# Which slots of a 128-slot tile the tokens of an expert take

## The reference

```python
g_idx = argmax(h @ w_grp + b_grp)                 # one of 4 groups for a token
e_prob = softmax(expert logits of that group)     # 8 experts in a group
top_p, top_local = lax.top_k(e_prob, 2)           # two experts for a token
order = jnp.argsort(expert); xs = h[order // 2]
a = ragged_dot(xs, w1, sizes); b = ragged_dot(xs, w3, sizes)
y = ragged_dot(silu(a) * b, w2, sizes) * weights[order][:, None]
return segment_sum(y, order // 2, num_segments=N) # each token gets its two rows back
```

## Time and profile before

| | us |
|---|---|
| median of three runs | 3200.97 |
| profiled execution | 3206.26 |
| its span, first to last instruction | 3204.0 |
| expert tiles within it, from the first gather to the end | 2560 to 3204 |

### The profile page before, as it was taken

One profiled execution on the slowest core, in us unless ns is written; L12 is line 12 of the kernel. 1 busy time (PEld: TensorE's weight loads), 2 busy tenths in 40 slices (PEclk: granted clock), 3 DMA queues, 4 the chain that ended last, 5 costly groups with the idle time before them and its releaser, 6 DMA issues. The chain is left out here.

```text
span 3204.0 us, 35751 instructions
## 1 busy us (share of the span) xinstructions
PE 2786.6 (87%) x13124; PEld 2228.3 (70%) x13124; DVE 2194.8 (69%) x2950; ACT 1271.2 (40%) x2069; POOL 858.3 (27%) x398
## 2 busy tenths in 40 slices
PE   6999999979588879789889968879599589999998
PEld 3777777755366668668777846768487478877776
DVE  5599975526698845844626978852544479888887
ACT  3222221110267621122324115666322167777775
POOL 1432310000111100001200025454321036776674
PEclk9999999989788889889999989989799589999999
DMA  6333347634455361235543255120532389999996
GB/s 217 99 109 116 106 162 250 200 120 141 152 188 187 128 246 53 87 99 118 118 120 76 76 130 101 38 50 18 219 118 93 132 313 380 364 362 355 365 360 218
DMA packets 244344, 543.37 MB, mean 170 GB/s; under 512 B 31109, under 2 KB 153973, under 8 KB 227906
## 3 DMA queue, kind: packets, MB, share of 16 engines
q1 hardware_dynamic: 174034, 436.42, 39.3%
q0 software_dynamic: 33840, 59.49, 7.4%
q10 hardware_dynamic: 36288, 45.09, 4.0%
HBM read 450.68 MB, written 108.06 MB: 174 GB/s over the span
## 5 line engine op out<-in xcount | busy, mean ns | idle before, releaser
L2548 DVE TENSOR_TENSOR e_low<-e_raw,e_high 128x4096 fp32r<-128x4096 f32 x99 | 441.7, 4463 | 87.5 <-ACT e_high L2542 87.4
L2542 ACT ACTIVATE e_high<-e_raw 128x4096 fp32r<-128x4096 f32 x99 | 359.5, 3634 | 138.0 <-DMA e_raw<-in_exp_w 111.0
L135 PE MATMUL banks<-h_high,w 128*128 128x512 f32 (+1 forms) x1088 | 309.1, 368 | 9.1 <-POOL w L364 4.4
L135 PE MATMUL banks<-p_w_high,p_high 128*128 128x512 f32 (+1 forms) x640 | 250.7, 392 | 14.7 <-DVE p_w_low L1593 14.7
L135 PE MATMUL banks<-p_w_low,p_high 128*128 128x512 f32 (+1 forms) x640 | 246.9, 386 | 0.0
L135 PE MATMUL banks<-p_w_high,p_low 128*128 128x512 f32 (+1 forms) x640 | 246.6, 385 | 0.0
L135 PE MATMUL banks<-e_high,e_xhigh 128*128 128x512 f32 x528 | 213.5, 404 | 26.4 <-issue 24.4
L135 PEld LDWEIGHTS banks<-h_high,w 128*128 128x128 f32 x1088 | 195.5, 190 | 48.6 <-POOL w L364 4.8
L495 DVE SCALAR_TENSOR_TENSOR acc<-img,taps,acc 128x1024 f32<-128x1024 f32 x160 | 209.8, 1311 | 5.7
L135 PE MATMUL banks<-e_high,e_xlow 128*128 128x512 f32 x528 | 208.5, 395 | 0.0
L135 PE MATMUL banks<-e_low,e_xhigh 128*128 128x512 f32 x528 | 208.0, 394 | 0.0
(11 more groups left out here) (501 smaller groups left out, 6598.3 us busy)
## 6 DMA issues: line engine op xcount, KB each, us to landing
e_raw<-in_exp_w SPq DMA_DIRECT2D x99, 2048.0 KB, 16.2
s_sums<-cumT SPq DMA_DIRECT2D x32, 768.0 KB, 4.4
w_raw<-in_w_in SPq DMA_DIRECT2D x20, 1024.0 KB, 6.6
s_X<-xtok SPq DMA_DIRECT2D x19, 1024.0 KB, 7.7
p_raw<-in_w_in SPq DMA_DIRECT2D x18, 1024.0 KB, 7.0
xbcT<-res ACTq DMA_DIRECT2D x20, 640.0 KB, 2.9
xtok<-xt ACTq DMA_DIRECT2D x20, 640.0 KB, 4.1
w_raw<-in_ada_w SPq DMA_DIRECT2D x12, 1024.0 KB, 5.4
```

What stands on the lines that cost most here:

```text
L135: last = pe.matmul(out, a, b, start=start and n == 0, stop=stop and n == len(pairs) - 1)
L2542: act.activation(self.high[p % HIGHS][:], self.raw[p % RAWS][:], ACT.Copy).then_inc(*self.high_done.up())
L2548: dve.tensor_tensor(self.low[p % HIGHS][:], self.raw[p % RAWS][:], self.high[p % HIGHS][:].bitcast(F32), ALU.subtract).then_inc(*self.low_ ...
```

## The change

A new row of 128 constants, `spread`, comes from memory to all partitions with the three others, and `here` compares it with `row_of` in place of the counting row. `spread[f(r)] = r`, where f(r) = 8 (r mod 16) + (r // 16 + (r mod 16) // 2) mod 8. So the token of rank r goes to partition f(r): ranks 0, 1, 2, 3, ... go to 0, 8, 17, 25, 34, 42, 51, 59, 68, ... Sixteen tokens that follow each other lie in sixteen different blocks of 8 partitions. The list, the slot weights, the gather and the scatter all go by the same `here`. The counting row is now only needed for tile numbers, and shrinks from 128 to 48 columns (`tile_numbers`).

```diff
+            "spread": np.argsort(8 * (k % 16) + (k // 16 + k % 16 // 2) % 8).astype(np.float32),
...
-        bgr, bex, cst, rows_in = rows
+        bgr, bex, cst, spread, rows_in = rows
...
-        token_no, token, line = new("token_no", NT), s.sb("r_token", [P, NT], I32), s.sb("r_line", [P, P], I32)
-        row_no = new("row_no", P)
+        token_no, token, line = new("token_no", NT), s.sb("r_token", [P, NT], I32), s.sb("r_line", [P, SLOT_TILES], I32)
+        tile_numbers = new("tile_numbers", SLOT_TILES)
...
-        pool.iota(line[:], [[1, P]], base=0, channel_multiplier=0).then_inc(*numbered.up())
+        pool.iota(line[:], [[1, SLOT_TILES]], base=0, channel_multiplier=0).then_inc(*numbered.up())
...
-        dve.wait_ge(*rows_in.at(3))
+        dve.wait_ge(*rows_in.at(4))
...
-        done(dve.tensor_copy(row_no[:], line[:]))
+        done(dve.tensor_copy(tile_numbers[:], line[:]))
...
-            done(dve.tensor_tensor(there[:, some, :], over(row_no[:, 0:SLOT_TILES], 1, NT), over(tile_of[:, j, :], 2, SLOT_TILES), ALU.is_equal))
+            done(dve.tensor_tensor(there[:, some, :], over(tile_numbers[:], 1, NT), over(tile_of[:, j, :], 2, SLOT_TILES), ALU.is_equal))
...
-            dve.tensor_tensor(here[:, some, :], over(row_no[:], 1, NT), over(row_of[:, j, :], 2, P), ALU.is_equal).then_inc(*placed.up())
+            dve.tensor_tensor(here[:, some, :], over(spread[:], 1, NT), over(row_of[:, j, :], 2, P), ALU.is_equal).then_inc(*placed.up())
...
+        spread = s.sb("r_spread", [P, P])
...
-            for to, name in ((bgr, "router_b_grp_2"), (bex, "router_b_exp_2"), (cst, "counts")):
+            for to, name in ((bgr, "router_b_grp_2"), (bex, "router_b_exp_2"), (cst, "counts"), (spread, "spread")):
```

More of the change, by code:

```diff
@@ L2820, in late @@
         slot_there = flat2(g)[:, 0:2 * NT * SLOT_TILES].rearrange("p (a n) -> p a n", n=SLOT_TILES)
-        route(core, dram, tables, (bgr, bex, cst, rows_in), lambda: [weights.fetch(m, j, m) for m, j in weights.order[0:3]], here, slot_there, weighed)
+        route(core, dram, tables, (bgr, bex, cst, spread, rows_in), lambda: [weights.fetch(m, j, m) for m, j in weights.order[0:3]], here, slot_there, weighed)
         experts(core, dram, tables, weights, y, g, dram["mod2"][0, 5 * D:6 * D], weighed)
```

## The result

The changed kernel takes 3176.3 us, the median of four runs (3173.68 to 3181.36), against 3201.6 us for four runs of the kernel before. The ratio is 0.9923, 95% interval 0.9906 to 0.9940. The forecast was 3177.5 us.

A forecast was written before the change was run, and what follows sets the result against it. DMA was taken to bound 23 of the 33 tiles, TensorE the rest. Terms -25.1 + 2 - 0.5 = -23.6 us, from 3201.0, gave 3177.4, stated as 3177.5; range 3174 to 3182, chance 0.66.

The forecast's parts named there:

- 23 tiles: Expert tiles from about 2731 us on: each goes from DMA's 18.86 us to TensorE's 17.77, -25.1 us.
- Eight engines carry the rows, and the excess in the shares is waiting: Expert tiles: eight engines carry all gathered and scattered rows; 8.7% excess in the weights' queue is waiting, not slower memory.
- Which group belongs to which engine: Token places: four partitions and four 32 further on give 17.81 us a tile after the change, 18.86 before.
- The price of a token: Gather and scatter: one row each per token, 0.525 us of engine time together, the empty slots' share included.
- pieces that come late: Weight pieces in the expert tiles: some late by a little, +2 us, bounds 0 and 6.
- last scatter: End of the kernel, tile of 7 tokens: two rows fewer in sequence, -0.5 us, bounds 0 and 1.3.
- fourth row, shorter counting row: Constants load and routing: the extra row is covered, the shorter row's saving lost in a wait; 0 us.
- the piece of lead in the raw buffers: First seven DMA-fed tiles: the piece in the raw buffers gives 7.6 us of lead, paying for DMA slightly over TensorE.
- Memory as the limit, hard or at 370 GB/s: Expert tiles: hard limit, no change, 3201, within a shared chance of 0.08; at 370 GB/s 3189, chance 0.09.
- Two engines still bound: Expert tiles: the fullest engine differs from tile to tile and still sets the pace; 3181 to 3187, chance 0.12.
- Partitions dealt out in turn: Token places: partitions go to engines in turn, so no change, 3201; within a shared chance of 0.08.
- The scatter's landing as the bound: Expert tiles: the next scatter waits for a landing that grows to 19.0 us; slower, 3213, chance 0.05.

The follow-up runs named there:

- e1: The changed kernel with the constants row holding 0, 1, 2, ..., so tokens fill partitions 0 to n - 1 as before; ratio to the kernel before 1.0003.
- e3: The changed kernel with places even by the rule of four partitions and four 32 further on; ratio to the kernel before 0.9921.
- d1: The changed kernel without low-part expert products, low part formed for half a piece, tokens in count order as before the change; 3194.1 us.
- d3: The changed kernel without low-part expert products, low part formed for half a piece, places even by four and four 32 further on; 3129.6 us.
- e2: The changed kernel without the rotation, rank r going to partition 8 (r mod 16) + r // 16; 3196.2 us, ratio to the kernel before 0.9978.
- d4_no_rows: The changed kernel without low-part expert products, low part formed for half a piece, every slot marked empty so no row moves; 3071.7 us.
- d2_change: The changed kernel, its token order kept, without low-part expert products and with the low part formed for half a piece; 3163.6 us.
- e4_no_rows: The changed kernel with every slot marked empty, so gathers and scatters move no row, all TensorE work kept; 3176.21 us, ratio 0.9907.

## Why the prediction was right

*What bounds.* DMA bounded 23 tiles at 18.86 us and TensorE would bound them at 17.77. After the change the same 23 tiles take 17.77.

*Eight engines carry the rows, and the excess in the shares is waiting.* The first part is shown by e1 to e3 and by d1 to d3, where only places differ. The second is shown by d1 to d3 as well: with the same bytes the recorded time of a weight row falls from 0.678 us to 0.620 when the rows are spread, and weights alone have 0.619. The prediction's count of it, from the kernel before alone, holds.

*Which group belongs to which engine.* The prediction took four partitions and four 32 further on, by a difference of 0.1 us for a tile. That was thin: with eight in a row the first sum would have been 18.97 against a measured 18.86. e2 and e3 separate the two rules by 20 us of the kernel's time in opposite directions, and both came out as this one says. The Trainium skill, page "DMA: Bandwidth & Descriptors", section "The descriptor swizzle", gives this rule for a transfer to 128 partitions, and all orders tried here agree with it for indirect ones. No run tries gather and scatter apart, but 0.52 us for a token is the recorded time of both its rows.

*The price of a token.* The 0.525 us hold the empty slots too. In d4_no_rows these take 1.1% of 16 engines, or 0.16 us a tile whatever the order, which is about what 14.90 us lie above the 14.77 of the prediction. The two small errors, a floor too low and a price too high, nearly cancel in the sums.

*The sum.* The stage from ScalarE's first weight piece went from 646.6 us (2557.38 to 3204.0) to 620.2 (2552.35 to 3172.5), so by 26.5, and the medians by 25.3. Term by term:

| term | predicted | measured |
|---|---|---|
| 23 tiles | -25.1 | -25.1 |
| pieces that come late | +2 | 0 |
| last scatter | -0.5 | -0.9 |
| fourth row, shorter counting row | 0 | 0 |
| before the first full tile | 0 | -0.5 |

The +2 was the one guess, and it was not needed. DMA alone takes 17.90 us in the change's order (d2_change), 0.13 over TensorE, which is 2.9 us in 22 tiles; the piece of lead in the raw buffers covers that. The lead can be followed in the change. Weight pieces land later after their issue in the middle of the tiles (2900 to 2950 us) than at their start (2610 to 2660):

```profile
e_raw<-in_exp_w SPq DMA_DIRECT2D x9, 2048.0 KB, 9.9
```

```profile
e_raw<-in_exp_w SPq DMA_DIRECT2D x9, 2048.0 KB, 12.2
```

In e4_no_rows it is 9.7 and 8.8 us in the same stretches, so it is the rows that use the lead up. After that it rises no more (12.0 us from 3050 to 3100), and no piece came late. Fuller tiles, or more of them, might show the 0.13 us; no run here has them. Here e3_by_fours would have room of 1.1 us for a tile and the change none. The 5 us by which the profiled spans differ beyond this lie ahead of the stage, where both kernels run the same instructions. The kernel by fours, with the change's code, has its first L2621 at 2589.9 us, the change at 2584.2 and the kernel before at 2589.5, so that part is scatter between executions.

*The rivals.* Memory as the limit, hard or at 370 GB/s: out (d3, d4). Two engines still bound: out for the kernel, though 17.90 shows how near it was. Partitions dealt out in turn: out (e1, which that rule would put at TensorE's 17.77 us a tile). The scatter's landing as the bound: it fell from 16.7 to 16.0 us, as forecast, and GpSimd's wait for it was 4.8 us in four places. With e3_by_fours that wait was 8.5 us in seven places, and still cost nothing. But the size of the landing was misread. I took it for turns behind weight packets and for rows. The last section shows that some 3.5 us of it are GpSimd's own, and in d4_no_rows a scatter that moves no row still lands 10.4 us after its issue at the median, against 12.4 in d2_change.

## What to carry to other kernels

An indirect DMA with many empty rows loads only the engines whose partitions hold the full ones; beside a stream that needs all 16, the fullest engine sets the pace, and spreading the rows costs one row of constants. Here that was 18.93 us a tile with 7.8 tokens on the fullest engine and 16.68 with 4.3. Check the order against the rule of four and four 32 further on: an order that was even in blocks of eight still used half of the engines for a tile of up to 64 tokens, and gained 0.2% instead of 0.8%. A DMA share of 0.98 is no proof of full engines, since e4_no_rows shows 0.96 at 83% of the rate: divide the GB/s by the rate in a stretch where nothing else runs.

## What the hardware showed beside this

GpSimd takes 5 us to issue a scatter beside VectorE's subtraction over 4096 columns, and 1.59 us when that is out of its way. Timeline of the changed kernel:

```profile
2806.67 4.42 DVE L2549 TENSOR_TENSOR e_low<-e_raw,e_high 128x4096 fp32r<-128x4096 f32 x1 [0.46 <-ACT e_high L2543]
2807.59 4.97 POOL L2680 DMA_INDIRECT result<-e_y,ids  x1 [0.89 <-POOL e_y L2676]
```

and of d2_change, where the subtraction is half as long and the issue falls between two of them:

```profile
2810.29 2.29 DVE L2549 TENSOR_TENSOR e_low<-e_raw,e_high 128x2048 fp32r<-128x2048 f32 x1 [2.70 <-ACT e_high L2543]
...
2814.61 1.59 POOL L2680 DMA_INDIRECT result<-e_y,ids  x1 [0.88 <-POOL e_y L2676]
2816.49 2.29 DVE L2549 TENSOR_TENSOR e_low<-e_raw,e_high 128x2048 fp32r<-128x2048 f32 x1 [3.25 <-ACT e_high L2543]
```

The scatters of that stretch of d2_change, duration and landing:

```profile
L2680 POOL DMA_INDIRECT result<-e_y,ids x22: 1588/1592/1595, 2743.9 to 3120.9; - x22
...
DMA to landing us min/median/max: 11.6/12.4/12.9
```

The issue never takes more than 1.6 us there, and the median landing falls from 16.0 to 12.4 us, though DMA is as full as before. In the changed kernel the issue ends at 2812.56 us, 1.47 us after the end of the subtraction (2811.09), so nearly a whole undisturbed issue lies behind that end. It looks blocked rather than slowed. The Trainium skill, page "SBUF — State Buffer", section "SBUF: two separate sides", tells of a port pair that VectorE and GpSimd share under an exclusive lock. By that section an operation of VectorE with two inputs in SBUF, as this subtraction is, holds it only against a GpSimd operation that reads SBUF. The times agree with such a lock if the issue reads `ids` from SBUF while it runs, but no run here took the lock away by itself. With TensorE as the bound it costs nothing.
